# A two-layer streaming encoder on one core: two full tiles and nine seven-product pairs in the first half of each feed-forward layer, and the forget gate in four column groups from the unrounded source

## The reference

```python
h = rms_norm(x, g) * (1.0 + scale) + shift        # scale, shift differ for prompt and sample
# forgetting attention (layer 1)
q, k, v, g, f = split_cols(h @ w_in, (1024, 1024, 1024, 1024, 16))
logf = log_sigmoid(f + b_forget)
cum = cumsum(concat([past_logf, logf]))            # past only for the sample
logit = q @ k.T * HEAD_DIM ** -0.5 + (cum_q - cum_keys)
o = (softmax(causal(logit)) @ v) * sigmoid(g)
x = x + gate1 * (o @ w_out)
# feed-forward, width 2816
gate, up = split_cols(h @ w_ffn_in, (2816, 2816))
x = x + gate2 * ((silu(gate) * up) @ w_ffn_out)
```

## Time and profile before

| what | value |
|---|---|
| median of 3 runs | 1533.2 us (1532.76 to 1535.65) |
| the profiled execution's own time | 1533.63 us |
| its span, first to last instruction | 1531.5 us |
| TensorE busy | 1492.0 us (97%), 11405 matmul records |
| VectorE, ScalarE, GpSimd busy | 1069.4, 634.3, 580.4 us |
| mean granted TensorE clock | 0.992 |
| DMA | 189.21 MB, mean 124 GB/s |

### The profile page before, as it was taken

How to read it: one execution, slowest core, us unless ns; L and a number is a source line. 1 busy time by engine, 2 the same in 40 slices (tenths; PEclk the granted TensorE clock), 3 DMA queues, 4 the chain that set the end, 5 groups by cost and what they waited for, 6 DMA issues and landing times.

```text
span 1531.5 us, 29136 instructions
## 1 busy us (share of the span) xinstructions
PE 1492.0 (97%) x11405; PEld 1373.2 (90%) x11405; DVE 1069.4 (70%) x2057; ACT 634.3 (41%) x1265; POOL 580.4 (38%) x346
## 2 busy tenths in 40 slices
PE   5999999999999999999999999999999999999998
PEld 2768956899999999999888888887999999999998
DVE  1659888668887778876644444457988877688753
ACT  3434366344552145522533333334254541355423
POOL 1234841225771066722322222231227640376421
PEclk8999999999999999999999999999999999999999
DMA  9874510341344433452254444443532355333521
GB/s 335 269 264 150 141 39 2 96 114 40 104 128 159 148 83 89 116 173 67 77 167 127 127 127 127 127 128 100 171 91 56 93 168 167 86 108 83 156 79 62
DMA packets 244454, 189.21 MB, mean 124 GB/s; under 512 B 12888, under 2 KB 228608, under 8 KB 240112
## 3 DMA queue, kind: packets, MB, share of 16 engines
q1 hardware_dynamic: 231232, 178.61, 38.9%
q10 hardware_dynamic: 13104, 8.97, 1.9%
HBM read 175.44 MB, written 8.50 MB: 120 GB/s over the span
## 4 chain that ended last, share of the span: by engine, by line
PE 86%; DVE 7%; ACT 3%; issue 2%; DMA 1%; POOL 0%; ACTq 0%; SPq 0%; POOLq 0%; DVEq 0%
PE lin L860 40%; PE lin L1440 28%; PE lin L877 5%; PE S L1201 2%; PE O L995 1%; PE O L1331 1%; PE O L1254 1%; DVE acc_out L2666 1%; PE T L1234 1%; PE S L1064 1%; DMA ada_raw<-in_w_ada 1%; PE S L1120 1%; ACT act_hi L1665 1%; PE lin L1300 1%; PE T L1291 0%
## 5 line engine op out<-in xcount | busy, mean ns | idle before, releaser
L2147 POOL TENSOR_TENSOR w_lo<-w_raw,w_hi 128x1024 fp32r<-128x1024 f32 (+3 forms) x68 | 168.3, 2476 | 409.6 <-ACT w_hi L1612 409.6
L2238 POOL TENSOR_TENSOR w_lo<-ada_raw,w_hi 128x512 fp32r<-128x512 f32 x114 | 156.9, 1378 | 241.8 <-ACT w_hi L1913 241.8
L1612 ACT ACTIVATE w_hi<-w_raw 128x1024 fp32r<-128x1024 f32 (+2 forms) x110 | 125.2, 1139 | 224.7 <-PE lin L860 212.3
L860 PE MATMUL lin<-act_hi,w_hi 128*128 128x288 f32 (+1 forms) x1088 | 164.6, 302 | 5.3 <-ACT act_hi L1644 2.0
L860 PE MATMUL lin<-act_hi,w_lo 128*128 128x288 f32 (+1 forms) x1088 | 167.3, 299 | 0.2
L860 PEld LDWEIGHTS lin<-act_hi,w_hi 128*128 128x128 f32 (+1 forms) x1088 | 149.5, 189 | 15.5 <-issue 10.1
L860 PE MATMUL lin<-act_lo,w_hi 128*128 128x288 f32 (+1 forms) x1088 | 162.1, 298 | 0.0
L860 PEld LDWEIGHTS lin<-act_hi,w_lo 128*128 128x128 f32 (+1 forms) x1088 | 149.9, 188 | 7.5 <-issue 6.7
L860 PEld LDWEIGHTS lin<-act_lo,w_hi 128*128 128x128 f32 (+1 forms) x1088 | 149.6, 188 | 3.4 <-issue 2.9
L2238 POOL TENSOR_TENSOR w_lo<-s_tmp,w_hi 128x512 fp32r<-128x512 f32 x76 | 129.2, 1717 | 15.0 <-ACT w_hi L1916 15.0
L1440 PE MATMUL lin<-act_hi,w_hi 128*128 128x288 f32 x608 | 105.4, 295 | 0.0
(11 more groups left out here) (347 smaller groups left out, 3031.1 us busy)
## 6 DMA issues: line engine op xcount, KB each, us to landing
ada_raw<-in_w_ffn_in SPq DMA_DIRECT2D x76, 512.0 KB, 5.2
w_raw<-in_w_ffn_out SPq DMA_DIRECT2D x32, 704.0 KB, 4.9
ada_raw<-in_w_ada SPq DMA_DIRECT2D x20, 1024.0 KB, 7.6
ada_raw<-in_w_ada SPq DMA_DIRECT2D x32, 512.0 KB, 5.0
w_raw<-in_w_in_b SPq DMA_DIRECT2D x32, 512.0 KB, 4.2
w_raw<-in_w_in_a SPq DMA_DIRECT2D x16, 512.0 KB, 6.2
ada_qo<-in_w_ada SPq DMA_DIRECT2D x8, 1024.0 KB, 7.5
ada_raw<-in_w_ada_final SPq DMA_DIRECT2D x16, 512.0 KB, 5.6
```

The source lines that it names most:

```text
L860: last = nc.tensor.matmul(lin_u(u)[0:m, tok], w, (lo if p == 2 else hi)[:, at(t) if at else t, tok], start=(p == 0 and t == 0), stop=(p == ...
L1612: A(w_hi[:, u % 2, 0:n], w_raw[:, u % 2, 0:n], ACT.Copy).then_inc(whi_done, 1)
L2147: TT(w_lo[:, u % 2, 0:n], w_raw[:, u % 2, 0:n], w_hi[:, u % 2, 0:n].bitcast(F32), ALU.subtract)\
L2238: TT(ring(w_lo, q), raw, ring(w_hi, q).bitcast(F32), ALU.subtract).then_inc(ws_lo_p, 1)
```

## The change

`FULL` becomes 2, so there are two full tiles and nine pairs in the first half of both layers. On VectorE the differences are made in the order 0, 1, 3, 2, and difference 2 stands between the sums S2 and S3; S1's rest and the last full tile's gate follow it. ScalarE and GpSimd follow that order, and the ring of weight slots is laid out anew.

The unit `U_FG` goes. Its weights are loaded into a 32 column wide buffer filled with zeros (`wf`, a part of `ada_row`), and `forget_gate` multiplies `fo`, the normed and scaled source before shift and rounding, in plain fp32: 16 matmuls of 32 rows and 288 columns in four column groups, and 8 of two columns for the shift's part, which goes into the bias. ScalarE adds the bias in three pieces over 128 partitions, and the fold over the four groups is done by the product with `fold_w` that also transposes. The running sums are taken per block alone, VectorE adds each block's start from the last column of the block before (`carry_on`), and they stand behind four steps of the unit U_B+3. The first turn of the attention loop is written out; in its first step the first 36 of the next unit's 48 matmuls stand ahead of `t_unit`.

```diff
-FULL = 3
+FULL = 2
 U_F0B = U_F0 + 2 * FULL + KT
-U_FG = U_F0B + KT
-U_B = U_FG + 1
+U_B = U_F0B + KT
...
-            at += n in ((2, 3, 5, 6), (2, 4, 6))[h % 2]
+            at += n in ((3, 6), (2, 4, 6))[h % 2]
...
@@ SP @@
-            w_load(U_FG, wb[:, 4096:4112], KT, 16)
+            sp.wait_ge(wf_zero, 1)
+            sp.dma_start(wf[:, :, 0:16], wb[:, 4096:4112].rearrange("(t p) n -> p t n", p=P)).then_inc(wf_in, 16)
...
@@ TensorE @@
+            def forget_gate():
+                pe.wait_ge(wf_in, 16)
+                pe.wait_ge(y_done, y_base(2, 1) + KT)
+                for r in range(2):
+                    for h in range(2):
+                        for j in range(4):
+                            kt = 4 * r + j
+                            nc.tensor.matmul(S[32 * j:32 * j + 32, h, 0:HALF], wf[:, kt, :],
+                                             fo[:, kt, h * HALF:(h + 1) * HALF], start=(r == 0), stop=(r == 1))
+                for r in range(2):
+                    for j in range(4):
+                        kt = 4 * r + j
+                        last = nc.tensor.matmul(S[32 * j:32 * j + 32, 0, HALF:HALF + 2], wf[:, kt, :],
+                                                mods[:, SHIFT[2] + kt, :], start=(r == 0), stop=(r == 1))
+                last.then_inc(fg_done, 1)
-            first_units(U_FG, 16, 2, ACT_N2)
-            pe.wait_ge(lin_free[U_FG % 2], free_count(U_FG))
+            first_units(U_B, P, 2, ACT_N2, forget_gate)
+            pe.wait_ge(z_done, 1)
             t_use(T_LF)
...
-                last = nc.tensor.transpose(T[:, t * 16:(t + 1) * 16], zb[:, c:c + P], ident[0:16, 0:16])
+                last = nc.tensor.matmul(T[:, t * 16:(t + 1) * 16], zf[:, c:c + P], fold_w[:, 0:16], start=True, stop=True)
...
-                    last = nc.tensor.matmul(S[0:16, 0, b * P:NP_], lf_tok[:, b, :], sums_w[:, 0:NP_ - b * P],
-                                            start=(b == 0), stop=(b == 3))
+                    last = nc.tensor.matmul(S[0:16, 0, b * P:(b + 1) * P], lf_tok[:, b, :], sums_w[:, 0:P],
+                                            start=True, stop=True)
...
-            lin_part(U_B + 1, None, KT, P, act_hi, act_lo, some=LIN_STEPS[0:18])
-            running_sums()
-            lin_part(U_B + 1, None, KT, P, act_hi, act_lo, some=LIN_STEPS[18:])
             linear(U_B + 2)
             k_tokens(0, 0, U_B + 1, T_B0)
...
             gate_steps(0, 4)
+            running_sums()
...
+                        ahead = first and r == 0 and k == 0
+                        if ahead:
+                            lin_part(u, 0, KT, P, act_hi, act_lo)
+                            lin_part(u, 1, KT, P, act_hi, act_lo)
                         t_unit(k, 0, r, n, t, it, 8, 26, pr_b, ps_b)
...
-            with pe.Fori(0, PAIRS // 2 - 1) as it:
+            b_body(0, False, True)
+            with pe.Fori(1, PAIRS // 2 - 1) as it:
                 b_body(it, False)
@@ ScalarE @@
-                for j in (0, 2, 1):
-                    t_hi(layer, j)
-                in_tile(u0, base, 1, lambda: split_hi(u0 + 4, N))
-                split_hi(u0 + 5, N)
+                t_hi(layer, 0)
+                t_hi(layer, 1)
 
                 def first_parts():
                     hi_part(n0, W_S1)
                     hi_part(n0, W_A11)
+                    t_hi(layer, 2)
+                    hi_part(n0, W_S2)
 
-                in_tile(u0, base, 2, first_parts)
-                hi_part(n0, W_S2)
+                in_tile(u0, base, 1, first_parts)
                 hi_part(n0, W_S3)
@@ GpSimd @@
-                pool.wait_ge(th_done, 4 * layer + (1 if j == 0 else 3))
-                pool.wait_ge(t_raw, 4 * layer + (3 if j == 0 else 4))
+                pool.wait_ge(th_done, 4 * layer + 1 + j)
+                pool.wait_ge(t_raw, 4 * layer + 2 + j)
@@ VectorE @@
+                def first_sums(n, between=None):
                     dve.wait_ge(t_free, T_ADA3 if n < N_A else T_H[(0, 5, 6)[half_of(n) - 1]] + 1)
-                    for i in (W_S1, W_S2, W_S3, W_S4):
-                        s_add(n, i)
-                    lo_part(n, W_S1)
+                    s_add(n, W_S1)
+                    s_add(n, W_S2)
+                    if between is not None:
+                        between()
+                        lo_part(n, W_S1)
+                        full_gate(1)
+                    s_add(n, W_S3)
+                    if between is not None:
+                        t_lo(layer, 2)
+                    s_add(n, W_S4)
+                    if between is None:
+                        lo_part(n, W_S1)
                 t_part(layer, nz, 0)
                 full_gate(0, NB)
-                t_part(layer, nz, 2)
+                t_part(layer, nz, 1)
                 full_lo(0)
-                t_part(layer, nz, 1)
                 t_part(layer, nz, 3)
-                t_lo(layer, 2)
-                full_gate(1)
-                full_lo(1)
                 if layer == 1:
                     sum_mods(5)
-                first_sums(n0)
-                full_gate(2)
-                full_lo(2)
+                first_sums(n0, lambda: t_part(layer, nz, 2))
+                full_lo(1)
...
+            for c in range(1, 4):
+                carry_on(0, c * P, (c + 1) * P, 0)
```

More of the change, by code:

```diff
@@ L961, in first_units @@
                     half_part(u + 1, 1, KT, P, act_hi, act_lo, [(0, kt)])
+                if late is not None:
+                    late()
                 for p in (1, 2):
@@ L1577, in b_body @@
                         pv_unit(k, n, PAIRS + r, t + 1, it, 8, 26, pT_b, pTs_b, vS_b[:, r, :, :], True)
-                        for half in range(2 if nxt else 0):
+                        for half in range(2 if nxt and not ahead else 0):
                             if k == 2:
@@ L2247, in pair_stage @@
             def pair_stage(n0, n1, u_out):
-                for i in (W_A11, W_S2, W_S3):
+                for i in (W_S2, W_S3):
                     lo_part(n0, i)
@@ L2263, in ffn_stage @@
                     split_lo(u, N)
-                for j in range(2):
-                    t_lo(layer, j)
+                t_lo(layer, 0)
+                t_lo(layer, 1)
+                lo_part(n0, W_A11)
                 pair_stage(n0, n0 + N_A, U_OUT[2 * layer])
                 out_stage(U_OUT[2 * layer], 0)
+                lo_part(n0 + N_A, W_A11)
                 pair_stage(n0 + N_A, n0 + N_ALL, U_OUT[2 * layer + 1])
@@ L2272, in _ @@
             pool.wait_ge(out_sent, 16 * 6)
+            nc.gpsimd.memset(wf, 0.0).then_inc(wf_zero, 1)
             out_stage(U_OA, N, 1)
-            ffn_stage(0, KT * 16, 2)
-            for c in range(5):
+            ffn_stage(0, N, 2)
+            for c in range(1, 5):
                 split_lo(U_B + c, N)
@@ L2949, in _, with carry_on @@
             dve.wait_ge(cum_done, 1)
-            chain(V.tensor_scalar(cum[:, 0:NP_], S[0:16, 0, 0:NP_], -1.0 / QSCALE, None, ALU.mult))
+            def carry_on(bank, c0, c1, at):
+                before = cum[:, at + c0 - 1:at + c0].broadcast_to([16, c1 - c0])
+                chain(V.scalar_tensor_tensor(cum[:, at + c0:at + c1], S[0:16, bank, c0:c1], -1.0 / QSCALE, before,
+                                             ALU.mult, ALU.add))
+            chain(V.tensor_scalar(cum[:, 0:P], S[0:16, 0, 0:P], -1.0 / QSCALE, None, ALU.mult))
+            for c in range(1, 4):
+                carry_on(0, c * P, (c + 1) * P, 0)
             dve.wait_ge(cum_done, 2)
-            chain(V.tensor_scalar(cum[:, NP_:], S[0:16, 1, 0:PAST + NS], -1.0 / QSCALE, None, ALU.mult))
+            chain(V.tensor_scalar(cum[:, NP_:NP_ + P], S[0:16, 1, 0:P], -1.0 / QSCALE, None, ALU.mult))
+            carry_on(1, P, 2 * P, NP_)
+            carry_on(1, PAST, PAST + NS, NP_)
             assert steps[0] == LF_CUM
```

70 lines of the change are left out of this document (39 added, 31 removed).

## The result

The changed kernel takes 1546.73 us (median of 4 runs, 1546.02 to 1548.17) against 1533.39 before: a ratio of 1.0088, 95% interval 1.0076 to 1.0100, 13.3 us slower. The forecast was 1547. The profiled execution has a span of 1544.3 us, 12.8 more than before, at a granted clock of 0.989.

What follows compares the result with a forecast made beforehand. TensorE, busy 97% of the span, was taken as the bound. 1533.6 + 6.0 (layer 0) + 6.8 (layer 1) + 2 (clock) - 1.1 (forget gate) = 1547.3; the median lies 0.4 lower, so 1547 us, range 1533 to 1552.

Steps and rivals of the forecast that it cites:

- the main mechanism: First pairs, both layers: VectorE instructions with two SBUF sources wait for GpSimd's running one; layers cost +6.0 and +6.8 us.
- The cover: First pair, layer 0: with one full tile fewer, TensorE waits 4.7 us for S1's low part, behind difference 2.
- The start-up wait: First pair, layer 0: the first product starts 0.5 to 0.8 us late, waiting for ScalarE's rounded S1; 0.8 was taken.
- Later waits in the first pair: After S1's low part, VectorE work meets GpSimd low parts; three later products together wait 2.1 us a layer.
- Layer 1: First pair, layer 1: sum_mods lets GpSimd's second T_lo go first, S1 comes 2.7 us later; +6.8 us in all.
- Clock: Waits in the first pairs bring TensorE's half clock for about 7 us; +2 us in all, ends 0 and 7.
- Forget gate: Removed unit and cheaper gate work save TensorE 4.7 us, of which 1.1 us is kept: -1.1 us.
- what is late next: Behind the forget gate: cumulative sums at 764.5, TensorE waits 2.7 us before transposes, U_B+5's late load; 0.5 to 1.7 us kept.
- more: Rival, 5%: clock falls in both layers and the attention's first turn, or column groups run in sequence (+4.9); 1552 to 1557.
- no waits: Rival, 12%: GpSimd's T_lo and low parts do not hold VectorE up, first pairs start on time; 1527 to 1529.
- half of it: Rival, 9%: only one T_lo is in the way, waits of 2 to 3 us a layer; 1534, range 1531 to 1537.

Runs made afterwards that it cites:

- ffn_only: The kernel before with only the feed-forward part of the change (two full tiles, new engine orders), old forget gate: 1542.11 us, ratio 1.0059 to before.
- forget_only: The changed kernel with three full tiles and the old feed-forward orders, so only the forget gate's part: 1536.11 us, ratio 1.0022 to before.
- t_lo_held: The changed kernel with both T_lo of GpSimd held back until difference 2 is written, VectorE's program unchanged: 1548.35 us, ratio 1.0103 to before.
- t_lo_memset: The changed kernel with GpSimd's two T_lo per layer replaced by a memset of the same tile to zero: 1537.25 us, ratio 1.0028 to before.
- wait_filled: The changed kernel with 24 more matmuls per layer, repeating the first product's first pass during TensorE's wait: 1548.63 us, ratio 1.0101 to before.
- the 8 bytes: New tile bias_z shifts the hid, Z and T tiles; with it in the forget gate's scratch, a kernel with three full tiles and a mended forget gate takes 1527.13 us.

## Why the prediction was right, and where it was not

The time was right (1547 for 1546.73), and so was the main mechanism. That the time came out within 0.3 us is luck: the feed-forward part was forecast 5.5 us too dear (14.8 for the 9.3 of ffn_only), the forget gate's part 4.0 too cheap (-1.1 for the 2.9 of forget_only).

- **The cover.** "TensorE, done with the first pass at 366.0, waits 4.7 us": it waited 4.03, to 370.2, for the instruction named, for the reason named. The start-up wait was 0.16 for the 0.8 expected. The blocking was worked out from the right rows, and t_lo_held and t_lo_memset bear it out.
- **Later waits in the first pair.** "2.1 us" a layer; 0.56 in layer 0 and none that lasts in layer 1. The step "each with two SBUF sources meets a GpSimd low part" failed: S3, T_lo 2, S4, hid_lo and the next S1 went through at 0.6 to 1.3 us each, and it was GpSimd's low part that waited, 4.35 us for work of 1.29, behind four instructions of VectorE in a row. The view of GpSimd's w_lo from 371 to 377 (durations in ns, shortest, median, longest):

```profile
L2268 POOL TENSOR_TENSOR w_lo<-s_tmp,w_hi x2: 1286/2816/4347, 371.4 to 375.7; 128x512 fp32r<-128x512 f32 x2
```

- **Layer 1.** "S1 comes 2.7 us later" failed: VectorE's S1 started at 1152.79 and GpSimd's T_lo at 1152.82, so VectorE was first by 0.03 us, and the first wait is 0.34 us instead of 3.5. I had put the 2.7 us of who gets in first wholly on one side; no run here has GpSimd in first, so what it would have cost stays an estimate.
- **Clock.** "+2 in all" was 4.3: 1.6 in layer 0 and 2.7 in layer 1. Waits of 16.0 us were forecast, 9.1 came. With the clock the feed-forward part was forecast at +14.8 and is -3.2 + 9.1 + 4.3 = 10.2 by the trace, 9.3 by ffn_only. The 4.3 is no price that could be saved alone: in wait_filled the waits grew by about what the clock gave back.
- **Forget gate.** "-1.1" was +2.9. TensorE's work fell by more than I took: the column-group sets take 2.2 us with the shift's, not 3.0, fold (1.03) and sums (1.63) as forecast. What failed is "what is late next". I had VectorE's chain hidden; the memset held it for 3.4 us, and cum was written at 772.50, 1.5 us behind the forecast's 764.5 moved by layer 0's 6.5. The first transposes came in time even so (784.20, forecast 784.5), with TensorE's 2.7 us of waiting spread over the sums (1.65) and the transposes (0.56). The load of U_B+5, which stands behind cum, was named as the last to come, and came at 792.1 where my numbers and the 6.5 us give 789.5 to 790.8. The half clock behind that wait (1.2 us on the first 16 matmuls of U_B+5) was not in the sum, only in the rival "more". And 2.1 us come from the 8 bytes, which no step of mine held.
- **One gain by chance.** From the sums of the norm ahead of layer 1's feed-forward layer to its units the changed kernel is 1.5 us faster, since the clock falls less there; no run tests why. The stretch in before, then in after (length; busy us of PE, PEld, DVE, ACT, POOL; granted clock, DMA share, GB/s):

```profile
1106.80:1134.90 28.10, 27.50 (x182) 26.86 (x180) 24.07 (x64) 16.52 (x36) 4.81 (x3) 0.88 0.45 125
```

```profile
1114.60:1141.20 26.60, 26.00 (x182) 25.36 (x181) 24.36 (x64) 16.53 (x36) 4.78 (x3) 0.94 0.50 134
```

By stages in the profiled executions: +6.5 to the norm ahead of layer 1's attention, +1.4 to the norm ahead of its feed-forward layer, -1.5 to that layer's units, +6.5 to the end, in all 12.8 with rounding.

Of the rivals, "no waits" and "half of it" are out, although in layer 1 VectorE did get its instruction in first. The clock's condition of "more" came true, it fell in both layers and in the attention's first turn (0.89 from 785 to 800), but its 1552 to 1557 did not, since the waits were 6.9 us shorter than forecast. What was not tried: giving GpSimd's T_lo to no one, that is, a third pass on unrounded sums, and why the half clock lasts four groups in one layer and six in the other.

## What to carry to other kernels

Before taking away work that covers others, add up what VectorE and GpSimd read with two SBUF operands until the next deadline as if it were one engine's; if the sum is over, another order may not save it (three did not here), and a wait that is mended can turn up a product or more later. When a unit is removed, look at every in-order queue whose next load stood behind the chain that is now shorter on TensorE, and pay for the clock behind each wait. Put new small tiles where they move nothing.
